# The first stage of a two-layer kernel rebuilt, and weight splits called ahead of unsplit blocks

## The chip, the cores and the metric

One core of a Trainium2 chip. The metric is the device time of one execution of the program in microseconds, the median of several runs. The kernel before takes 2598.72 us (three runs, 2596.58 to 2601.68).

## What is computed

Two transformer layers run one after the other over 512 tokens of width 1024, in float32. Only the start and the middle of the first layer matter here:

```python
mod = jax.nn.silu(c) @ w_ada[l] + b_ada[l]          # c: 1 x 1024, w_ada: 1024 x 6144
shift1, scale1, gate1, shift2, scale2, gate2 = jnp.split(mod[:, None, :], 6, axis=-1)
h = rms_norm(x, norm1_w[l]) * (1 + scale1) + shift1
proj = h @ w_in[l]                                   # split into q, k, v, z, alpha, beta, mla_*, gates
...
o_b = mla_attention(mla_q, mla_ckv, mla_kr, ...)     # keys and values from ckv @ w_uk, ckv @ w_uv
y_b = o_b.reshape(B, S, MLA_VD) @ w_out_mla[l]
```

The first 24 column blocks of `proj` (q, k and v of 8 heads, 128 columns each) go through a short causal convolution and silu into a gated delta rule; alpha and beta are its gates. MLA is latent attention: its keys and values come from a 256-wide latent through `w_uk` and `w_uv`. The rest of layer one (output products, gated FFN) and layer two follow.

## The kernel before

**Layout.** Activations lie channel-major: a tile is 128 channels x 512 tokens, 2 KB per partition, in an SBUF arena of 57 such tiles. A product of one output tile of 128 channels takes, for each of the eight 128-row slices k of the weight block, three TensorE matmuls in fp32r (`mm3`): weights and input are each split into a high half (rounded to fp32r) and a low half (the rest), and hi x hi, hi x lo and lo x hi are summed in PSUM. One block of 128 columns is 24 matmuls of 128x512.

**Weight blocks.** A block is 128 x 1024 floats (512 KB). The sync engine (SP) loads the blocks in the order of one list, `W.list`, into three raw slots (`RAW`). For a split block ScalarE copies raw to `WHI` (a 128x1024 activation), and VectorE (odd list numbers) or GpSimd (even ones) writes the difference to `WLO`; both have three buffers. A raw slot is free again when the low half is made. Some blocks are not split: 32 pieces of `w_ada` for parts 2 to 5, used by VectorE, and `w_uv` (2) and `w_uk` (8, one for each head), used raw by TensorE; their slot is free when they have been used. The list is made by running the same program once with a planner (`Plan`). In it, numbers 0 to 4 are ab (k_rope, alpha, beta), dn0, dn8, dn16, dn1, then w_ada pieces and dn blocks alternate (number 10 is dn2). Later come z0 at 71, 72, then uv0, uv1 (73, 74), z0 75, 76, z1 77 to 79, uk0, uk1 (80, 81), z1 82, gd 83, 84, uk2, uk3 (85, 86), gd 87 to 92, gm 93, uk4, uk5 (94, 95), gm 96 to 102, uk6, uk7 (103, 104), and ya (`w_out_dn`) from 105.

**Who splits when.** Every engine runs the same program of stages, each with its own steps, in order. A linear stage calls `self.ahead(i)` for each of its blocks i before anything else; ScalarE, VectorE and GpSimd then split all blocks of the list up to number i + 2 that are not split yet (lines 1533, 2205, 2868). ScalarE waits there for the raw block, and for the buffer that the third split block before has used. Only linear stages and the w_ada stages call it; the MLA steps with uv and uk blocks don't.

**The first stage** (`prologue` of each engine, lines 1014, 1558, 2224, 2889, and `sync_program`, line 3127). SP loads two pieces of constants, parts 0 and 1 of w_ada whole (8 MB in four loads of 2 MB), a third piece of constants, some 30 small vectors as rows, and then the list. ScalarE's queue loads c and x (2 MB). TensorE transposes x into eight channel-major tiles; VectorE copies each from PSUM (`XT`), ScalarE squares it, VectorE adds the squares; one product with ones gives the sum over channels, ScalarE takes its inverse root; GpSimd multiplies all eight tiles by it. VectorE takes silu(c) @ w_ada for parts 0 and 1 with 32 multiply-adds of 128x512, and `ada_end` sums over partitions on TensorE with 16 products by a column of ones. Then for each k the scaled and shifted tile is made (ScalarE for even k, VectorE for odd), split by ScalarE (high) and VectorE or GpSimd (low), and TensorE runs its first k-loop over two blocks at once, ab and dn0:

```python
lin("ab", w_in, 8, 0, 256, H1, lambda m: ("dn_ve", 0) if m else ("ab_act", "kr"), fresh=True, ...)
```

`fresh` makes the first two blocks of a linear stage share one k-loop, so that TensorE follows the input tiles as they are made. Behind it ScalarE splits block 3 and evicts ab (`ab`, `gates_ab`), convolutions and silus follow (`dn_conv`, `dn_taps`, `dn_silu`), then the loop over the other q, k and v blocks. ScalarE writes `XT` to memory (`xs1`) for the residual sum.

**The MLA part.** `beside` (linear stages z0, z1, gd, gm, gates, `split_o`, ya) is woven with `norms_then`: `mla_norms` with the uv products and the norms and rotations of q and k, then the heads in pairs (`mla_head`). A head's first step is its uk product on TensorE, a Square of it on ScalarE, an add on VectorE; its second is a product with ones, then logarithm, exponential and the scores. `split_o` makes the high and low halves (`HO`) that ya reads.

Of the kernel before, what the change touches and what calls it, by code (L numbers as in the profile page):

```python
# [7 lines left out]
P = 128  # L8
# [208 lines left out]
class Lin:  # L217


    def __init__(self, name, w, kn, c0, ncol, X, freed, m0=0, r0=0, parts=None, fresh=False):  # L220
# [65 lines left out]
def build(nc, D, out, known):  # L286
# [5 lines left out]
    with ctx:  # L292
# [90 lines left out]
        ADA0 = [A[:, 21 + 16 * i:37 + 16 * i, :].rearrange("p (k a) n -> p k (a n)", k=8) for i in range(2)]  # L383
# [24 lines left out]
        colpos, row_loads = {}, []  # L408
        g_, r_ = 0, 0
        for name, src, n, new in vectors:  # L410
# [3 lines left out]
            if name in ("qr", "kr"):  # L414
                row_loads += [(ROW[g_][r_:r_ + 1, 64 * hh:64 * hh + 64], src) for hh in range(2)]
            else:
                row_loads.append((ROW[g_][r_:r_ + n, :], src))
            r_ += n
# [47 lines left out]
        H1 = Split("h1", HP, lambda k: "po" if k % 4 == 1 else "ve")  # L466
# [21 lines left out]
        def lin(name, *a, **kw):  # L488
            L[name] = Lin(name, *a, **kw)

        lin("ab", w_in, 8, 0, 256, H1, lambda m: ("dn_ve", 0) if m else ("ab_act", "kr"), fresh=True,
            parts=lambda g: [(rows(w_in, 0, 8, MR, 64), 0), (rows(w_in, 0, 8, 4096, 32), 64),
                             (rows(w_in, 0, 8, 4104, 32), 96)] if g == 0 else [(rows(w_in, 0, 8, 0, P), 0)])
        for c in range(1, 24):
# [7 lines left out]
        lin("z0", w_in, 8, 3072, 512, H1, lambda m: ("z_ve", m))  # L502
        lin("z1", w_in, 8, 3584, 512, H1, lambda m: ("z_ve", m), m0=4)
        lin("gd", w_in, 8, GD, 1024, H1, lambda m: ("gd_ve", m))
        lin("gm", w_in, 8, GD + 1024, 1024, H1, lambda m: ("gm_ve", m))
        lin("ya", D["w_out_dn"][0], 8, 0, 1024, HO, lambda m: ("ya_ve", m))
        lin("yb", D["w_out_mla"][0], 8, 0, 1024, OB, lambda m: ("yb_ve", m), fresh=True)
        lin("wo", D["w_o"][0], 8, 0, 1024, HM, lambda m: ("r1_ve", m), fresh=True)
        lin("ple", D["w_ple_2"][0], 2, 0, 1024, PP, lambda m: ("ple_act", m))
        up_ = D["ffn_w_up"][0]  # L510
        lin("fu0", up_, 8, 0, 256, H2, lambda m: ("fv_ve", 0) if m else ("fa_ve", 0), fresh=True,
# [4 lines left out]
        lin("fd", D["ffn_w_down"][0], 22, 0, 1024, FP, lambda m: ("r2_ve", m))  # L516
        SU, SV, GQ, GK, GV, GR, GA, AQ, AK, AV, CA, CG = 0, 512, 1024, 1280, 1536, 2048, 2560, 2576, 3088, 3600, 4112, 4624
        lin("cv0", w2, 8, 0, 256, H3, lambda m: ("ca_ve", 0) if m else ("cg_act", 0), fresh=True,
# [5 lines left out]
        lin("aq", w2, 8, AQ, 512, H3, lambda m: ("aq_act", m))  # L524
        lin("ak", w2, 8, AK, 512, H3, lambda m: ("ak_act", m))
        lin("ga", w2, 8, GA, P, H3, lambda m: ("ga_act", m))
        lin("gk", w2, 8, GK, 256, H3, lambda m: ("gk_act", m))
        lin("gq", w2, 8, GQ, 256, H3, lambda m: ("gq_act", m))
        lin("gr", w2, 8, GR, 512, H3, lambda m: ("gr_act", m))
# [5 lines left out]
        lin("w2", D["w_out_2"][0], 8, 0, 1024, HG, lambda m: ("r3_ve", m), fresh=True)  # L535
        for p in range(4):
            lin(f"up{p}", D["w_ff1_2"][0], 8, p * 1024, 1024, H4, lambda m, p=p: ("f2_ve", p, m), fresh=p == 0)
            lin(f"do{p}", D["w_ff2_2"][0], 8, 0, 1024, F2[p], lambda m, p=p: ("r4_ve", p, m), r0=8 * p)
        lin("pg", D["w_ple_gate_2"][0], 8, 0, 1024, H5, lambda m: ("pg_ve", m), fresh=True)
# [34 lines left out]
        def ADA_SUM(p):  # L574
            return [A[:, 53, :], A[:, 54, :]] if p == 1 else [SCR[3], SCR[4]]
# [70 lines left out]
        class Stages:  # L646
# [47 lines left out]
            def ev_ab(self, m, bk):  # L694
                if m:
                    self.ev_dn(0)(m, bk)
# [2522 lines left out]
```

## Time and profile before

| | |
|---|---|
| median of three runs | 2598.72 us |
| the profiled execution | 2600.64 us, its span 2598.7 us |
| mean granted clock of TensorE | 0.942 of 2.4 GHz |
| busy: TensorE, VectorE, ScalarE, GpSimd | 2343.5, 1103.9, 928.4, 732.1 us |

The span goes from the first instruction to the last; some 2 us of the execution lie around it. PE is TensorE's matmuls, PEld its weight loads, DVE VectorE, ACT ScalarE, POOL GpSimd; SPq and ACTq are the queues that issue DMAs. `ps` is a PSUM bank, `wraw`, `whi`, `wlo` the weight buffers, `hhi`, `hlo` the input halves, `arena` and `scr` other tiles. Lines such as L342, L357 or L360 are helpers that issue every matmul, activation or tensor-tensor operation. In an arrow `a <- b` after an idle time, b is what the instruction waited for. A granted clock of 1.00 is 2.4 GHz, 0.50 is 1.2 GHz.

### The profile page before, as it was taken

To read this page: it belongs to the slowest core of one execution; us is meant where nothing else is said; L and a number is where in the kernel's file an instruction comes from. 1 tells how busy PE (TensorE), PEld (TensorE's weight loads), DVE (VectorE), ACT (ScalarE), POOL (GpSimd) and SP (SyncE) were. 2 spreads that over 40 slices of the span, in tenths; PEclk is the share of its full clock that TensorE was granted. 3 is DMA by queue.
4 is the path that set the end of the run, shared out by engine and by line. 5 is a ranking of instruction groups with operands and counts; after the bars stand their busy time and mean duration, and the time that the engine had idled before them with its cause. 6 is when DMAs were issued, how large, how long until landed. Compare 5 with 4: busy or idle time off the path is not lost.

```text
span 2598.7 us, 26841 instructions
## 1 busy us (share of the span) xinstructions
PE 2343.5 (90%) x10834; PEld 1895.1 (73%) x10834; DVE 1103.9 (42%) x1605; ACT 928.4 (36%) x1353; POOL 732.1 (28%) x427
## 2 busy tenths in 40 slices
PE   2788989997879989899999897999998999999996
PEld 2677877994457767688888685787776777888875
DVE  5466656444332333333331299613444243332333
ACT  2444424213342433433332332324553433422334
POOL 4341144101201025422232314221132343422332
PEclk6898989998889989999999898999999999999998
DMA  6321223131112123333333331232222322333331
GB/s 234 93 70 57 82 57 85 62 92 38 36 41 59 31 81 114 106 97 98 97 93 97 111 105 57 73 98 82 73 74 63 100 89 82 106 96 94 103 120 51
DMA packets 345822, 220.64 MB, mean 85 GB/s; under 512 B 18281, under 2 KB 327132, under 8 KB 345700
## 3 DMA queue, kind: packets, MB, share of 16 engines
q1 hardware_dynamic: 335940, 200.26, 26.5%
q10 hardware_dynamic: 9760, 18.67, 2.2%
q8 instruction: 87, 1.43, 0.2%
q14 instruction: 35, 0.29, 0.0%
HBM read 210.49 MB, written 8.41 MB: 84 GB/s over the span
## 4 chain that ended last, share of the span: by engine, by line
PE 74%; DVE 11%; ACT 8%; POOL 4%; issue 2%; DMA 1%; ACTq 0%; SPq 0%; DVEq 0%; POOLq 0%
PE ps L342 73%; DVE arena L368 4%; ACT arena L357 3%; DVE arena L360 2%; POOL arena L360 2%; ACT scr L357 1%; DVE scr L368 1%; ACT whi L357 1%; ACT L353 1%; POOL wlo L360 1%; PE ps L345 1%; DVE wlo L360 1%; DVE arena L365 1%; DMA arena<-in_x_dram 1%; DVE arena L371 0%
## 5 line engine op out<-in xcount | busy, mean ns | idle before, releaser
L342 PE MATMUL ps<-hhi,whi 128*128 128x512 f32 x1664 | 679.5, 408 | 81.0 <-POOL wlo L360 49.1
L360 POOL TENSOR_TENSOR wlo<-wraw,whi 128x1024 fp32r<-128x1024 f32 (+1 forms) x164 | 393.9, 2402 | 1144.2 <-ACT whi L357 1144.2
L342 PE MATMUL ps<-hlo,whi 128*128 128x512 f32 x1664 | 663.6, 399 | 0.0
L342 PE MATMUL ps<-hhi,wlo 128*128 128x512 f32 x1664 | 663.2, 399 | 0.0
L357 ACT ACTIVATE whi<-wraw 128x1024 fp32r<-128x1024 f32 (+1 forms) x328 | 340.8, 1040 | 375.6 <-PE ps L342 304.6
L342 PEld LDWEIGHTS ps<-hhi,whi 128*128 128x128 f32 x1664 | 323.2, 194 | 162.0 <-issue 78.2
L342 PE MATMUL ps<-arena 128*128 128x128 f32 (+4 forms) x2304 | 338.9, 303 | 42.1 <-ACT arena L357 17.8
L360 DVE TENSOR_TENSOR wlo<-wraw,whi 128x1024 fp32r<-128x1024 f32 x164 | 216.2, 1318 | 372.1 <-ACT whi L357 372.0
L342 PEld LDWEIGHTS ps<-hlo,whi 128*128 128x128 f32 x1664 | 323.3, 194 | 67.7 <-issue 2.9
L342 PEld LDWEIGHTS ps<-hhi,wlo 128*128 128x128 f32 x1664 | 321.4, 193 | 69.7
L342 PEld LDWEIGHTS ps<-arena 128*128 128x128 f32 x2304 | 290.8, 199 | 73.8 <-issue 21.7
L357 ACT ACTIVATE arena<-ps 128x512 f32<-128x512 f32 (+5 forms) x223 | 116.3, 540 | 350.3 <-PE ps L342 289.7
L342 PE MATMUL ps<-h,whi 128*128 128x512 f32 x512 | 160.3, 395 | 1.1 <-POOL wlo L360 1.1
L360 POOL TENSOR_TENSOR arena<-arena,scr 128x512 f32<-128x512 f32 x65 | 103.7, 1602 | 168.3 <-ACT scr L357 131.2
L368 DVE SCALAR_TENSOR_TENSOR arena<-arena,colv 128x512 f32<-128x512 f32 (+1 forms) x148 | 137.4, 935 | 30.4 <-ACT arena L357 26.7
L357 ACT ACTIVATE scr<-ps,colv 128x512 f32<-128x512 f32 x78 | 55.6, 712 | 253.4 <-PE ps L342 253.2
L368 DVE SCALAR_TENSOR_TENSOR scr<-ps,colv,scr 128x511 f32<-128x511 f32 (+2 forms) x116 | 86.9, 749 | 135.4 <-ACT scr L357 132.9
L360 DVE TENSOR_TENSOR arena<-ps,arena 128x512 f32<-128x512 f32 (+1 forms) x88 | 55.6, 639 | 149.8 <-PE ps L342 147.9
L360 DVE TENSOR_TENSOR scr<-ps,scr 128x512 f32<-128x512 f32 x86 | 59.1, 689 | 138.7 <-PE ps L342 137.1
L342 PE MATMUL ps<-arena,cst 128*128 128x512 f32 (+1 forms) x124 | 73.8, 725 | 45.5 <-ACT arena L357 18.9
L342 PEld LDWEIGHTS ps<-h,whi 128*128 128x128 f32 x512 | 97.3, 190 | 22.7 <-issue 2.6
L342 PE MATMUL ps<-ff,whi 128*128 128x512 f32 x352 | 108.4, 390 | 0.0
(192 smaller groups left out, 2680.8 us busy)
## 6 DMA issues: line engine op xcount, KB each, us to landing
wraw<-in_w_in_dram SPq DMA_DIRECT2D x99, 512.0 KB, 3.9
wraw<-in_w_ff_dram SPq DMA_DIRECT2D x64, 512.0 KB, 4.0
wraw<-in_ffn_w_up_dram SPq DMA_DIRECT2D x44, 512.0 KB, 3.9
wraw<-in_w_ada_dram SPq DMA_DIRECT2D x32, 512.0 KB, 4.0
wraw<-in_w_gate_dram SPq DMA_DIRECT2D x32, 512.0 KB, 3.6
arena<-in_w_ada_dram SPq DMA_DIRECT2D x4, 2048.0 KB, 20.1
wraw<-in_ffn_w_down_dram SPq DMA_DIRECT2D x16, 512.0 KB, 3.7
wraw<-in_w_branch_dram SPq DMA_DIRECT2D x16, 512.0 KB, 3.4
```

What stands on the lines that cost most here:

```text
L342: return pe.e.matmul(o, l, r, start=start, stop=stop)
L345: return pe.e.transpose(o, i, CST[0:n, C_ID:C_ID + n])
L353: ac.e.preload_act_table_set("natural_log_exp_and_others")
L357: return ac.e.activation(o, i, f, bias=bias, scale=scale, **kw)
L360: return q.e.tensor_tensor(o, a, b, op)
L365: return q.e.tensor_scalar(o, a, s1, s2, op0, op1)
L368: return ve.e.scalar_tensor_tensor(out=o, in0=a, scalar=s, in1=b, op0=op0, op1=op1)
```

## The change

**The first stage.** x is loaded by SP right after the first constants, in four loads of 128 tokens, each with its own semaphore. The w_ada parts 0 and 1 are loaded in two halves of 4 MB (half s holds columns 512 s to 512 s + 511 of both parts, in four loads); the first three weight blocks lie between the halves, and the small vectors, the third piece of constants and the rest of the list behind them. The nine row vectors that stand in the first row tile (b_ada and norm weights; `row_group` 0) go over ScalarE's queue. The mean square is taken token-major: ScalarE squares x with an accumulated sum per token, and ScalarE and VectorE scale two token tiles each by the inverse root, in place. x is transposed twice: unscaled for the residual, scaled (`turn_x`) for the layer. VectorE's 32 multiply-adds and GpSimd's eight multiplications go; w_ada is multiplied on TensorE as rows (weights: one column of silu(c), 512 columns stream), copied by VectorE, and turned to columns by eight products with a 1x1 one. VectorE makes every shifted tile straight from PSUM and every low half. The first k-loop has three blocks (ab, dn0, dn8), and the second w_ada half and its turns lie inside it, before k = 4; the other four row tiles are turned before k = 6. Block 1's low half is made behind the first half's mod. The write of x to memory moves behind high half 3.

**Splits ahead.** `mla_norms` and `mla_head` of ScalarE, VectorE and GpSimd call `ahead` for their uv and uk blocks, so the two blocks behind are split before that step.

**Names.** Semaphores of one engine are merged (`on_act`, `zg_act`, `gt_act`, `gs_act` into `mix_act`, and others alike); their order is the program's.

```diff
-        first = 2 if self.fresh else 1
+        first = self.fresh or 1
...
-        H1 = Split("h1", HP, lambda k: "po" if k % 4 == 1 else "ve")
+        H1 = Split("h1", HP, lambda k: "ve")
...
-        lin("ab", w_in, 8, 0, 256, H1, lambda m: ("dn_ve", 0) if m else ("ab_act", "kr"), fresh=True,
+        lin("ab", w_in, 8, 0, 384, H1, lambda m: ("dn_ve", 8 * m - 8) if m else ("ab_act", "kr"), fresh=3,
...
...
+            def ada_half(self, s):
+                for p in range(2):
+                    bk = PA.take("ar", s, p)
...
+                    for k in range(8):
+                        pe.wait_ge(SG.sem(f"ada_in{s}{p}{k // 4}"), 16)
+                        t = mm(bk[0:1, :], SC[:, k:k + 1], ADA0[s][p][:, k, :], k == 0, k == 7)
...
+                self.turn_x(4 * s)
+                self.turn_x(4 * s + 1)
...
+                for p in range(2):
+                    pe.wait_ge(*at("row_ve", s, p))
+                    for c in range(4):
+                        t = mm(bk[:, 4 * p + c:4 * p + c + 1], ADA_ROW[p][:, c * P:(c + 1) * P], ones[0:1, 0:1], True, True)
...
+                self.turn_x(4 * s + 2)
+                self.turn_x(4 * s + 3)
+            def between(self, k):
+                if k == 4:
+                    self.ada_half(1)
+                if k == 6:
...
...
+                ve.wait_ge(*at("st_act", "ri"))
+                for b in (0, 2):
+                    ts(ve, X0[:, b, :], X0[:, b, :], RX[:, b:b + 1], None, ALU.mult).then_inc(*inc("st_ve", "x", b))
...
+                for s in range(2):
+                    self.first_mod(s)
+                    if s == 0:
+                        self.ahead(0)
+                    for k in range(4 * s, 4 * s + 4):
...
+                        ts(ve, HS[k % 3], PA.of("hx", k)[:, :], modcol(1, k), modcol(0, k), ALU.mult, ALU.add).then_inc(
...
+                        self.low(H1, k, HS[k % 3])
...
+                    act(SCRT[:, 2 * (b % 2):2 * (b % 2) + 2, :].rearrange("p a n -> p (a n)"), X0[:, b, :], ACT.Square,
+                        accum=SQ4[:, b:b + 1]).then_inc(*inc("st_act", "sq", b))
...
+                for b in (1, 3):
+                    act(X0[:, b, :], X0[:, b, :], ACT.Copy, scale=RX[:, b:b + 1]).then_inc(*inc("st_act", "x", b))
+                self.ahead(0)
...
+                for n in range(2):
+                    self.ahead(W.index["uv", n])
...
             def mla_head(self, h):
+                self.ahead(W.index["uk", h])
...
+            for b in range(4):
+                sp.e.dma_start(X0[:, b, :], D["x"][0, b * P:(b + 1) * P, :]).then_inc(SG.sem(f"x_in{b}"), 16)
+            load_ada(0)
+            for u in W.list[0:3]:
+                load_block(u)
+            load_ada(1)
```

## Rows read from the trace of the kernel before

**Rows 1.** The page, part 1: busy us (share of the span), instructions.
```profile
PE 2343.5 (90%) x10834; PEld 1895.1 (73%) x10834; DVE 1103.9 (42%) x1605; ACT 928.4 (36%) x1353; POOL 732.1 (28%) x427
```

**Rows 2.** Table of stretches: us, PE, PEld, DVE, ACT, POOL busy (instructions), granted clock, DMA share, GB/s.
```profile
0.00:66.00 66.00, 17.01 (x72) 14.59 (x72) 39.75 (x58) 15.25 (x21) 31.13 (x16) 0.68 0.68 230
...
80.00:121.00 41.00, 30.66 (x134) 24.78 (x134) 23.35 (x31) 19.73 (x28) 9.82 (x4) 0.89 0.29 86
...
600.00:925.00 325.00, 264.19 (x989) 179.39 (x988) 121.95 (x225) 127.46 (x225) 49.92 (x27) 0.88 0.16 44
...
925.00:2598.00 1673.00, 1570.26 (x6892) 1278.36 (x6890) 648.03 (x869) 600.42 (x835) 519.21 (x294) 0.97 0.31 91
```

**Rows 3.** Chain of waits, 0 to 140 us, the longest pieces: start us, us, what.
```profile
1.36 13.35 DMA arena<-in_x_dram
...
35.71 27.09 POOL arena L360 x8
...
66.72 12.60 PE ps L342 x45
...
120.38 8.29 PE ps L342 x24
```

**Rows 4.** The same table of stretches, short stretches.
```profile
24.00:27.00 3.00, 0.00 (x0) 0.00 (x0) 2.19 (x4) 0.71 (x2) 0.00 (x0) 0.50 1.03 410
...
40.00:44.00 4.00, 3.57 (x16) 3.48 (x16) 4.00 (x8) 0.06 (x1) 4.00 (x1) 0.50 1.09 297
...
105.70:111.10 5.40, 5.40 (x25) 4.50 (x24) 4.52 (x5) 2.14 (x3) 2.40 (x1) 1.00 0.01 3
```

**Rows 5.** Timeline, TensorE: start us, us, what, form, count.
```profile
14.75 6.25 PE L345 MATMUL ps<-cst,arena 128*128 128x128 f32 x32 [11.33 <-DMA arena<-in_x_dram]
...
40.23 3.57 PE L342 MATMUL ps<-cst,scr 128*128 128x1 f32 x16 [3.15 <-DVE scr L368]
```

**Rows 6.** Timeline, VectorE and GpSimd: a copy from PSUM, a low half.
```profile
15.90 0.69 DVE L371 COPY arena<-ps 128x512 f32<-128x512 f32 x1 [15.90 <-PE ps L345]
...
75.61 2.40 POOL L360 TENSOR_TENSOR wlo<-wraw,whi 128x1024 fp32r<-128x1024 f32 x1 [1.17 <-ACT whi L357]
```

**Rows 7.** TensorE's forms, 200 to 260 us: ns min/median/max, first and last start.
```profile
L342 PE MATMUL ps<-hhi,whi x32: 388/390/794, 199.8 to 259.7; 128*128 128x512 f32 x32
...
L342 PE MATMUL ps<-arena,cst x8: 593/593/593, 224.9 to 227.9; 128*128 128x512 f32 x8
```

**Rows 8.** Timeline, ScalarE behind the first two blocks.
```profile
79.41 1.06 ACT L357 ACTIVATE whi<-wraw 128x1024 fp32r<-128x1024 f32 x1 [3.87 <-PE ps L342]
...
93.17 1.15 ACT L357 ACTIVATE gb<-arena 40x512 fp32r<-40x512 f32 x2 [2.50 <-DVE arena L2294]
...
98.77 1.04 ACT L357 ACTIVATE whi<-wraw 128x1024 fp32r<-128x1024 f32 x1
```

**Rows 9.** Timeline, ScalarE, VectorE and the sync queue around the unsplit blocks.
```profile
616.70 1.23 DVE L360 TENSOR_TENSOR wlo<-wraw,whi 128x1024 fp32r<-128x1024 f32 x1 [5.92 <-ACT whi L357]
...
698.31 0.37 SPq L3146 DMA_DIRECT2D wraw<-in_w_in_dram  x1
...
700.52 1.05 ACT L357 ACTIVATE whi<-wraw 128x1024 fp32r<-128x1024 f32 x1
...
702.20 1.06 ACT L357 ACTIVATE whi<-wraw 128x1024 fp32r<-128x1024 f32 x1 [0.63 <-DMA wraw<-in_w_in_dram]
...
896.37 26.93 SPq L3146 DMA_DIRECT2D wraw<-in_w_out_dn_dram  x4
...
911.47 4.25 ACT L357 ACTIVATE hhi<-arena 128x512 fp32r<-128x512 f32 x8
```

**Rows 10.** Waits of TensorE, 600 to 930 us (us, times, longest); one from the timeline.
```profile
PE ps L342 <- DVE wlo L360: 14.5, 3, 9.5
...
PE ps L342 <- POOL wlo L360: 8.3, 2, 4.1
...
704.14 0.76 PE L342 MATMUL ps<-hhi,whi 128*128 128x512 f32 x1 [4.14 <-POOL wlo L360]
```

More of the change, by code:

```diff
@@ L811, in program @@
             first = f.qkv(more)
-            for _ in range(5):
+            for _ in range(4):
                 next(first)
@@ L1027, in prologue @@
                     PA.put(("xt", k), "st_ve", "xt", k)
-                bk = PA.take("ri")
-                pe.wait_ge(*PA.free("ri"))
-                pe.wait_ge(*at("st_ve", "sum", 7))
-                mm(bk[:, :], ones, SQT, True, True).then_inc(*inc("st_mm", "ri"))
-                PA.put(("ri",), "st_act", "ln")
-                pe.wait_ge(SG.sem("rows"), 16 * len(row_loads))
-                pe.wait_ge(*at("st_po", "rz"))
+                pe.wait_ge(SG.sem("rows0"), 16 * row_group.count(0))
@@ new lines, in turn_x @@
+            def turn_x(self, k):
+                bk = PA.take("hx", k)
+                pe.wait_ge(*PA.free("hx", k))
+                pe.wait_ge(*at("st_ve", "x", 2))
+                pe.wait_ge(*at("st_act", "x", 3))
+                for b in range(4):
+                    t = tr(bk[:, b * P:(b + 1) * P], X0[:, b, k * P:(k + 1) * P])
+                t.then_inc(*inc("st_mm", "h", k))
+                PA.put(("hx", k), "st_ve", "h", k)
+            def between(self, k):
+                if k == 4:
+                    self.ada_half(1)
+                if k == 6:
+                    pe.wait_ge(SG.sem("rows"), 16 * (len(row_loads) - row_group.count(0)))
+                    bk = PA.take("col1")
+                    pe.wait_ge(*PA.free("col1"))
+                    for i in range(4):
+                        t = tr(bk[:, i * P:(i + 1) * P], ROW[1 + i])
+                    t.then_inc(*inc("st_mm", "col1"))
+                    PA.put(("col1",), "st_ve", "col1")
@@ L2426, in mla_norms @@
                 for n in range(2):
+                    self.ahead(W.index["uv", n])
                     for p in SG.ends("rec"):
@@ L2965, in mla_norms @@
             def mla_norms(self):
-                for _ in range(8):
+                yield
+                yield
+                for n in range(2):
+                    self.ahead(W.index["uv", n])
+                    yield
+                for _ in range(4):
                     yield
@@ L2977, in mla_norms, with mla_head @@
                 yield
-            mla_head, o_norms, z_gate, gates = Plan.idle_head, Plan.o_norms, Plan.z_gate, Plan.gates
+            def mla_head(self, h):
+                self.ahead(W.index["uk", h])
+                for _ in range(11):
+                    yield
+            o_norms, z_gate, gates = Plan.o_norms, Plan.z_gate, Plan.gates
             def split_o(self):
@@ L3124, in ev_pg, with load_ada, load_block @@
                     self.add_square("pg", m, [A[:, 32, :], A[:, 33, :]])
+        def load_ada(s):
+            for p in range(2):
+                for g in range(2):
+                    sp.e.dma_start(ADA0[s][p][:, 4 * g:4 * g + 4, :],
+                                   rows(D["w_ada"][0], 4 * g, 4, p * 1024 + s * S, S)).then_inc(SG.sem(f"ada_in{s}{p}{g}"), 16)
+        def load_block(u):
+            if u["before"] is not None:
+                sp.wait_ge(*at(*raw_free(u["before"])))
+            v = raw_of(u["i"])[:, 0:u["kk"] * u["n"]].rearrange("p (k n) -> p k n", k=u["kk"])
+            for src, off in u["parts"]:
+                sp.e.dma_start(v[:, :, off:off + src.shape[2]], src).then_inc(SG.sem(f"raw{u['slot']}"), 16)
         def sync_program():
```

331 lines of the change are left out of this document (160 added, 171 removed).

## The prediction

> **What bounds the kernel now.** I read the engine table first: TensorE is busy 90% of the span, the next engine 42% [rows 1]. So a microsecond is only to be had where TensorE waits. The table of stretches says where that is: TensorE is busy for 17.0 of the first 66 us, 30.7 of the 41 us from 80 to 121, and 264 of the 325 from 600 [rows 2]. The change works in these stretches. The rest stays as it is, and moves as a block.
>
> In the first stage the chain of waits goes through the load of x (13.4 us), a ping-pong of copies, squares and sums, eight multiplications on GpSimd (27.1 us), and only at 66.7 us into the first product [rows 3]. The two blocks of the first k-loop end near 80.0 us (the row shows the first block's end; the second's last three matmuls come 0.7 us later). From there to the eleventh block (number 10 of the list) at 120.4 TensorE starts a block only when it has been loaded and split: a raw slot comes free, the block lands, is split, and only then used. So after the first stage the pace is that of load and split, and an earlier start moves this chain as a whole.
>
> **Part 1, the first stage, step by step.** x is alone at the head of the queue. The queue moves 410 GB/s in its 2 MB loads [rows 4], so 2.1 MB from about 3 us (the old x load began at 1.4 us; two constant loads and four issues lie ahead) are in at about 8.5 us, and the first half of w_ada (4.2 MB, 10.2 us) at 19; 10.7 by a shorter 2 KB row is no matter, as TensorE is later. The three weight blocks and the second half follow at 25 and 36 us. The 32 transposes took 6.25 us, but in the old ping-pong [rows 5]; unbroken copies of 0.69 us each [rows 6] don't hold them back, so 7 us: 15.5. The squares, the logarithm and the scaling (four passes of 1.05 us on ScalarE as the 128x1024 split, two on VectorE) end at 18.4, beside TensorE. The nine row loads now on ScalarE's queue, some 0.3 us each, are issued by 5 us and queue only ScalarE's first square behind them.
>
> TensorE then takes w_ada as 16 products of 128x512 for each half, 32 instructions. The nearest row is the ones product in full fp32: eight instructions starting 3.0 us from first to last, 0.43 us apart at 2.4 GHz [rows 7]; at 1.2 GHz, half of it, they are 0.86 apart, which is the other bound. I take 0.43, as the transposes ahead of them leave the engine busy: 13.7 us, to 29.5. Four transposes, eight column products and the row copies, as 16 instructions that took 3.57 us at 1.2 GHz [rows 5], halved, and 16 transposes: 3.9 us, to 33.4. VectorE's bias and gain (0.6), its split of block 1 (1.2) and the first turned block (product from PSUM 0.65, ScalarE 0.65, subtraction 0.7) put the first product at 36.5. Each k needs 9 matmuls, and 25 took 5.4 us [rows 4], 2.04 us, and on VectorE and ScalarE 2.09, so four take 8.2, plus 2.5 for a restart at half clock: 47.1. The second half lies on the path now, since TensorE is in order: 13.7 and 3.9 to 64.7, then 1.8 for the first block, four k of 2.09, and the 0.5 of the column transposes: 75.4, or 76 with some half clock. So **three blocks are done at 76, where two were done at 80.0**.
>
> What comes after loses part of that. ScalarE's split of block 3 started at 79.41, as the first pair's loop ended; the gates' work followed, and the split of block 6 came at 98.77 [rows 8]. Now there are two splits ahead of the gate work instead of one (1.05), and ahead of it too one more convolution with three taps on VectorE (2.3) and a silu that waits for them (1.9 with its table); 1.2 come back, as block 3 may be split 1.2 us before the loop ends. Worked through in ScalarE's order, block 6 is split 19.5 us after the loop, subtracted by 23.0 (2.4 on GpSimd [rows 6]), block 8 loads (4.5; such a load alone took 3.9 from issue to split [rows 9]), is split and subtracted by 31.0, and block 10 by 39.1: 115.1 us, against a start at 120.4 [rows 3]. **Part 1 gives 5.3 us**; the third block taken early buys nothing beyond, as it only fills the wait behind it. With the loop's end between 71 and 84 this is +10 to -3.
>
> TensorE's clock decides this part. In the stretch from 40 to 44 us it was busy 3.57 of 4 us with one-column products and stayed at the lower level, 1.2 GHz [rows 4]. The new row products are one column wide on the other side: their weights are a single column, and 512 columns stream. No row shows such a product. The Trainium skill, "TensorE: Matmul & The Clock Gate" (section on the HAM clock gate), says that the clock depends on how busy the engine has been, with the lower level as the default. By the page the sum has 13.7 us for a half; by the row from 40 to 44, if it is what counts, 27.3.
>
> **Part 2, splits ahead of unsplit blocks.** Five times between 600 and 925 us TensorE waits for a low half: 2.01, 4.14, 2.98, 4.15 and 9.52 us, three for VectorE's and two for GpSimd's [rows 10]. Each lies right behind a pair of unsplit blocks (w_uv, then w_uk of two heads): the split of the next block was asked for only by that block. The raw data was there: at the second wait ScalarE's split starts at 700.52 with no wait for a load [rows 9]. The new calls take it before the pair.
>
> First wait: the low half is made before the copies, TensorE starts at 608.9 and saves 2.0; VectorE then also waited 5.92 us, until 616.7, for the next block [rows 9], whose slot came free late. That slot is now free before the pair, so the copy behind the split, at 617.9, follows the product instead (608.9 + 5.5 = 614.4): **3.5**. Second: 4.1 for the wait and 1.8 for the restart at half clock (its first matmul took 0.76 us [rows 10], where the median is 0.39 [rows 7]): **5.9**. Third, which started nearly warm: **3.0**. Fourth: 4.15 and 0.7, **4.8**. Cost: in the second head of each pair ScalarE now waits for a block whose slot that pair frees (issued at 698.31, split from 702.20 [rows 9]) with its Square behind it; that is 3.2 us later, but TensorE has a block of 5.5 us to do meanwhile. At the fifth wait there is no such block: the load issued at 896.37 [rows 9] lands near 900.3, Square waits, and heads 6 and 7 lose 3.1 us. Then the eight highs that started at 911.47 [rows 9] start at 914.6, and the products of w_out_dn start behind the first low, near 916, and go at the pace of GpSimd's lows to 922.8. Before, that first block ran from 920.27 for 5.5 us and 1.8 of restart, to 927.6: **4.8** net. Together **22.0 us**.
>
> The merged semaphores (on, z, zg, gd, gm and so on) are counted by one engine in program order as before; they issue nothing new and cost nothing.
>
> What is moved past queues stays covered. The other small loads and the last 612 KB of constants now follow the second half on the sync queue and are in by some 42 us; GpSimd's two casts wait for them, and behind those only memsets that are due at 76. The write of x to memory leaves ScalarE's queue at the fifth block (some 43 us), holds one issue, and is due only when a silu first writes over x, past 90. Block 3's product needs a bank that ScalarE's copies free 4.6 us after the loop; its successor, block 6, waits for its split until 23 us, so this costs nothing unless that wait goes.
>
> **Sum.** 27.3 us off the profiled execution's 2600.64 gives 2573.3; it stood 1.9 us above the median of 2598.72, so the median goes to about 2572. Later stages are limited by TensorE (busy 1570 of 1673 us [rows 2]) and hide no earlier start.
>
> **Rivals.** *(a) The row products run at 1.2 GHz.* Two halves cost 27.3 instead of 13.7 us, and their transposes and column products 3.6 more each: 34 us, all on TensorE's path. Net +7: 2606. It decides when some four fifths of both halves run low. For it: the stretch from 40 to 44. Against: there the data streamed was one column in 0.22 us, here 512. *(b) ScalarE's new waits cost as much as they save.* Its queue is in order, so the wait for the second block's load delays both heads' exponentials; if TensorE's block does not cover it, the second to the fifth wait return half: 11 instead of 22, so 2583. *(c) The calls do nothing:* the slot or the high buffer is still taken when they are reached, and ScalarE stands there instead. Part 2 is nothing: 2593. Against it: the split at 700.52 waited for neither.
>
> **How the numbers follow.** Forecast 0.59, (a) 0.13, (b) 0.18, (c) 0.10. Part 1 between +10 and -3 and part 2 between 11 and 25 put the range at 2562 to 2590; with (c) and a part of (a)'s way it reaches 2594, and 2560 below. About 0.2% (5 us) is what a measurement of this kernel can tell from no change: faster 0.82, the same 0.06 (halves of (a) and (c)), slower 0.12.
>
> **What would show it.** Right: x landed by 9 us, first product near 36, a gap of some 18 us in the k-loop with 32 row matmuls 0.43 apart at a granted clock near 1, three blocks done near 76, block 10 near 115; no wait over 1 us for a low half behind uk or uv. Wrong: row matmuls 0.86 apart; first product after 45; Squares of odd heads late with TensorE waiting for them; or the five waits still there under another name.

## The result, and the profile after

The kernel after takes 2569.65 us (median of four, 2568.42 to 2577.01) against 2599.32 us (median of four) of the kernel before: the ratio is 0.9892, with a 95% interval of 0.9871 to 0.9913, so 29.7 us or 1.1% faster. The forecast was 2572, inside a range of 2560 to 2594. The profiled execution took 2570.07 us, with a span of 2568.3. Below it will turn out that the total is better than its parts: one part gave more than forecast, the other less.

The page, part 1, of the kernel after; it answers to [rows 1]:
```profile
PE 2358.6 (92%) x10928; PEld 1890.4 (74%) x10928; DVE 1083.0 (42%) x1579; ACT 927.7 (36%) x1352; POOL 700.4 (27%) x417
```
TensorE is busy for 15 us more and the span is 30 us shorter: the row products of w_ada are new work on the engine that bounds the kernel, put where it stood idle. The table of stretches of the kernel after shows where, against [rows 2] (us, then PE, PEld, DVE, ACT, POOL busy, granted clock, DMA share, GB/s):
```profile
0.00:66.00 66.00, 51.78 (x199) 26.07 (x200) 18.67 (x31) 16.12 (x23) 8.41 (x12) 0.93 0.79 254
...
595.00:892.00 297.00, 249.06 (x969) 171.57 (x968) 117.16 (x219) 125.97 (x224) 46.30 (x26) 0.91 0.18 46
892.00:2568.00 1676.00, 1568.58 (x6893) 1275.81 (x6891) 650.87 (x870) 600.43 (x834) 519.48 (x296) 0.97 0.31 90
```
In the first 66 us TensorE is busy for 51.8 instead of 17.0. From the first unsplit block to the products of w_out_dn the idle time falls from 61 to 48 us. The last stretch is as long as before, within 3 us.

The chain of waits of the kernel after, its long pieces in the first 120 us, answers to [rows 3]:
```profile
3.08 6.45 DMA arena<-in_x_dram
9.66 5.33 PE ps L345 x33
14.99 13.82 PE ps L342 x32
...
35.65 24.35 PE ps L342 x68
60.00 1.03 PE ps L345 x8
61.03 1.88 PE ps L342 x16
...
65.81 6.73 PE ps L342 x18
72.97 2.78 PE ps L342 x12
...
112.22 2.46 POOL wlo L360
114.82 5.74 PE ps L342 x24
```
Read it from the bottom. Block 10 starts at 114.82 where it started at 120.38, and its 24 products take 5.74 us where they took 8.29. Only the first of these two differences was in the forecast. TensorE's wait just ahead of the block is now short (timeline):
```profile
114.82 0.47 PE L342 MATMUL ps<-hhi,whi 128*128 128x512 f32 x1 [0.50 <-POOL wlo L360]
```

To follow a gain along the kernel I take the start of ScalarE's high half of a block in each trace and subtract that of the kernel before. For after: 5.7 us earlier at block 10, 8.1 at block 14, 8.7 at block 27, 10.1 at block 31, 13.0 at block 57, and 13.0 still at block 75, where the first unsplit block comes. From there it rises to 31.9 at block 109 and ends at 31.1.

### The profile page after: what moved, and what is told of

Read it like the earlier page. It is cut to its first block, busy times and chain, and to the rows that moved or that the text cites. A ratio compares the mean times of both kernels' runs of the same rounds, so it can differ in the third digit from the quotient of the medians.

```text
span 2568.3 us, 27012 instructions
## 1 busy us (share of the span) xinstructions
PE 2358.6 (92%) x10928; PEld 1890.4 (74%) x10928; DVE 1083.0 (42%) x1579; ACT 927.7 (36%) x1352; POOL 700.4 (27%) x417
## 4 chain that ended last, share of the span: by engine, by line
PE 75%; DVE 11%; ACT 8%; POOL 3%; issue 3%; DMA 1%; ACTq 0%; SPq 0%; DVEq 0%; POOLq 0%
PE ps L342 74%; DVE arena L368 4%; ACT arena L357 4%; DVE arena L360 2%; DVE scr L368 1%; PE ps L345 1%; ACT scr L357 1%; POOL wlo L360 1%; ACT whi L357 1%; ACT L353 1%; POOL arena L360 1%; DVE arena L365 1%; DVE scr L360 1%; DVE wlo L360 1%; DMA wraw<-in_w_in_dram 1%
## 5 line engine op out<-in xcount | busy, mean ns | idle before, releaser
L360 POOL TENSOR_TENSOR arena<-arena,scr 128x512 f32<-128x512 f32 x57 | 76.5, 1346 | 133.8 <-ACT scr L357 96.8
L342 PE MATMUL ps<-arena,cst 128*128 128x512 f32 (+1 forms) x122 | 70.1, 703 | 34.5 <-ACT arena L357 17.7
```

Of the source, the lines that this page charges most:

```text
L342: return pe.e.matmul(o, l, r, start=start, stop=stop)
L360: return q.e.tensor_tensor(o, a, b, op)
```

## The experiments

Expectations are quoted as they stood before each run. Medians are against runs of the kernel before on the same chip. Positions inside a kernel are from its one profile.

**1. The first stage alone.** The three classes lose their calls ahead of w_uv and w_uk:
```diff
-                    self.ahead(W.index["uv", n])
-                self.ahead(W.index["uk", h])
```


> The first stage alone: the kernel after, without the calls ahead of w_uv and w_uk. Theory G (the gain of the first stage grows behind block 10, because TensorE reaches block 10 almost without a stop and stays at 2.4 GHz): block 10 starts near 114.8 us, everything from about 450 us on is 13 us earlier than before, and the time is 12 to 13 us below before, near 2587. Rival F (the forecast's sum, in which the shift of the first stage stays 5.3 us, and what the traces show beyond it belongs to the calls or to chance): 5.3 us below before, near 2594. The waits for low halves between 600 and 925 us are there as before, 19 to 24 us in all by the profile's waits.

Measured: 2589.45 us against 2597.59; the ratio 0.9969 [0.9958, 0.9980] is 8 us, between 5 and 11. In the trace block 10 is 5.1 us earlier than before, block 14 7.6, block 57 12.5, block 109 13.7. So what grows behind block 10 belongs to the first stage, as theory G has it; the median of six runs gives 8, not the 13 of the profile. The 5.5 us between lie in which executions were profiled: that of before took 3.0 us more than the median of before here (2600.64 against 2597.59), and that of run 1 was the fastest of its six, 2.5 us below their median. Runs 11 and 12 show how two executions of one program come to differ by that much.

**2. The calls alone**, added to the kernel before.

> The calls ahead of w_uv and w_uk alone, in the kernel before. Theory G: nothing moves before 600 us, then 19 us are gained up to about 890 us: near 2580. Rival F: the forecast's 22 us or the 24 that are left of the measured gain when the first stage gives 5.3: 2575 to 2577. A third possibility is that the two parts are not additive (the calls profit from where the first stage puts the blocks): then less than 15 us, above 2584.

Measured: 2584.40 us, ratio 0.9949 [0.9936, 0.9962]: 13 us, between 10 and 17. In its trace nothing moves before 590 us (0.9 us later), and at block 109 it is 17.0 earlier: 17.9 from the calls. The medians of the two parts add up to 21.3 us, with some 3 us of uncertainty each, the whole measured 29.7 and 28.8. The traces show no piece that only both together give (after minus run 1 is 18.2 at block 109, run 2 gave 17.9), so I take the two parts as additive. The medians do not show it: they fall 7 to 8 us short of the whole, and that gap stays open.

**3. Two blocks in the first k-loop.**
```diff
-        lin("ab", w_in, 8, 0, 384, H1, lambda m: ("dn_ve", 8 * m - 8) if m else ("ab_act", "kr"), fresh=3,
+        lin("ab", w_in, 8, 0, 256, H1, lambda m: ("dn_ve", 0) if m else ("ab_act", "kr"), fresh=2,
...
-        for c in (*range(1, 8), *range(9, 24)):
+        for c in range(1, 24):
```


> The kernel after with only two blocks in the first k-loop; the third is an ordinary block behind it. The forecast's claim (the third block taken early buys nothing, since it only fills the wait for the split of block 6): block 10 starts within 1 us of 114.8, and the time is that of the kernel after within 2 us, near 2570. Rival: the third block's 24 products ride at the pace of VectorE inside the loop and cost TensorE nothing there, so as an ordinary block it costs its full 5.5 us behind the loop: near 2575; and if TensorE then comes late to block 10 the start moves to 117 or later.

Measured: 2571.24 us, ratio 0.9902 [0.9886, 0.9918], that of after within the intervals. The loop ends 3.4 us earlier, block 10 is split at 110.6 instead of 111.1. As far as the start of block 10 goes the forecast's claim holds: the third block taken early buys nothing there, because TensorE waits 4.16 us for block 6 in the kernel after. But it decides where TensorE waits. With two blocks in the loop the stop ahead of block 10 is back, and the clock with it (timeline of TensorE, run 3):
```profile
114.22 0.77 PE L342 MATMUL ps<-hhi,whi 128*128 128x512 f32 x1 [2.98 <-POOL wlo L360]
114.78 0.63 PE L342 MATMUL ps<-hlo,whi 128*128 128x512 f32 x1
```
The block's 24 products take 7.16 us here, 5.74 in the kernel after. From block 10 to block 14 the gain on the kernel before grows by 0.5 us in this run, and by 2.4 to 2.5 in all the executions of the six that run 11 lists. So this growth comes with the third block. What it is worth in the end is less: block 14 is 6.6 us earlier in run 3 and 7.1 in the mean of the six, and the medians cannot tell the two apart.

**4. Fourteen of the second half's row products left out.**
```diff
-                        t = mm(bk[0:1, :], SC[:, k:k + 1], ADA0[s][p][:, k, :], k == 0, k == 7)
+                        if s == 0 or k == 7:
+                            t = mm(bk[0:1, :], SC[:, k:k + 1], ADA0[s][p][:, k, :], k == 0 or s == 1, k == 7)
```


> The kernel after with only the last of the eight products for each part of w_ada in the second half (14 of 16 are left out, so the bias and gain of the last four blocks of x are wrong sums): 14 x 0.86 = 12.0 us less on TensorE in the gap of the first k-loop. The forecast's claim (the second half lies on TensorE's path, and the chain behind it moves as a whole): the loop ends near 64 us, block 10 starts near 103, and the time is 12 us below the kernel after, near 2558. Rival: the second half of w_ada lands and the splits of VectorE and ScalarE go at a pace of their own, so the loop ends only some 6 us earlier and the time is near 2564. Second rival: the loop ends 12 us earlier, but the loads of the blocks behind it, or ScalarE's gate work, hold the chain, and less than half of it reaches block 10.

Measured: 2557.84 us, ratio 0.9849 [0.9833, 0.9864]; 11.8 less than the kernel after. Block 3 is split 12.0 us earlier than in after (63.8 for 75.8), block 10 12.3 earlier. Both rivals fall. The row products are on the path that sets the stage, and the chain of load and split behind it moves as a whole.

**5. The odd head's call behind its norm.**
```diff
-                self.ahead(W.index["uk", h])
+                if e == 0:
+                    self.ahead(W.index["uk", h])
...
                 act(SCR[e], SCR[e], ACT.Exp, scale=-0.5).then_inc(*inc("ma_act", "ri", h))
+                if e == 1:
+                    self.ahead(W.index["uk", h])
```
and so behind KZ on VectorE.

> The kernel after, with the call ahead of w_uk of an odd head moved behind the exponential of its key norm (ScalarE) and behind the rotated key's product (VectorE), so that neither head's Square and logarithm wait for the next block's load. Forecast's mechanism (the call costs 3.1 us at heads 6 and 7; the trace of after shows ScalarE waiting 3.83 us for w_out_dn at 870.93 and TensorE 5.97 us behind it): everything from the first product of w_out_dn on is 3 to 4 us earlier than in the kernel after, near 2566.5, and TensorE's wait at 875 shrinks to 2 us or less. Rival: TensorE waits for the chain of norms of two heads anyway (with nothing else to do there), and the wait only changes its name: under 1 us, near 2570.

Measured: 2564.58 us, ratio 0.9860 [0.9845, 0.9874], 5.1 below after. What it removes stands in the kernel after, heads 6 and 7, timeline of TensorE and ScalarE:
```profile
864.59 3.60 PE L342 MATMUL ps<-arena,wraw 128*128 128x512 f32 x8
...
870.93 1.06 ACT L357 ACTIVATE whi<-wraw 128x1024 fp32r<-128x1024 f32 x1 [3.83 <-DMA wraw<-in_w_out_dn_dram]
871.89 0.58 ACT L357 ACTIVATE scr<-ps 128x512 f32<-128x512 f32 x1
...
875.01 2.07 PE L342 MATMUL ps<-scr,cst 128*128 128x512 f32 x2 [5.97 <-DVE scr L360]
```
ScalarE stands at the split of w_out_dn's block until it lands; head 7's Square (871.89) is behind it, and TensorE waits 5.97 us for what follows. The wait names VectorE's sum, but the DMA set it. In the timeline of run 5 the same product comes 1.58 us after the one of head 6, the Square at 866.87, the split at 871.51 without a wait:
```profile
866.67 1.02 PE L342 MATMUL ps<-scr,cst 128*128 128x512 f32 x2
868.25 1.12 PE L342 MATMUL ps<-scr,cst 128*128 128x512 f32 x2 [0.56 <-DVE scr L360]
```
The products of w_out_dn start 5.0 us earlier (882.69 for 887.68); relative to the blocks ahead of w_uv, where this run is 0.6 behind after, it is 6.2 ahead at block 109, and 2.0 of them are there by block 91, behind the third pair. The rival (only the name changes) falls.

**6. Eight row products of the second half ahead of the first k.**
```diff
             def ada_half(self, s):
-                for p in range(2):
+                for p in range(s, 2):
+                    self.ada_rows(s, p)
...
             def between(self, k):
+                if k == 0:
+                    self.ada_rows(1, 0)
```
`ada_rows(s, p)` is the eight products of one part with their bank.

> The kernel after, with the eight row products of the shift part of w_ada's second half (6.9 us) ahead of the first k instead of in the gap at the fifth. They fill TensorE's wait of 2.92 us for the first low half and keep it busy, so the first k steps run at 2.4 instead of 1.2 GHz. Theory (TensorE's path sets this stage): the first product starts near 39.6 instead of 35.65, k = 0 to 3 take 8.3 instead of 10.5 us, the loop ends 4 to 5 us earlier, and block 10 too: near 2565. Rival: the first four k go at the pace of VectorE and ScalarE (2.09 us each) and are not late at present, or the data of the second half is not there at 32.7: less than 1.5 us gained, near 2569, or a loss up to 3 us.

Measured: 2570.01 us, ratio 0.9876 [0.9859, 0.9892]: nothing gained. The loop ends 2.6 us earlier, and so is block 10 (2.4). Timeline of TensorE in this run:
```profile
34.46 8.35 PE L342 MATMUL ps<-arena,mod 128*1 128x512 f32 x16 [1.37 <-DVE scr L365]
42.73 0.50 PE L342 MATMUL ps<-hhi,whi 128*128 128x512 f32 x1
```
The products waited 1.37 us for a bank that VectorE frees, started at the lower clock (8.35 us instead of 6.9: the first instructions stand 0.81 to 0.85 us apart, those from the fifth on 0.43), and so put the first k at 42.7, not 39.6; from there the four k took the expected 8.3 us. The 2.4 us were lost again at places far behind: 1.2 at block 16, 1.6 at block 31, 2.8 at block 57. I had no reason for that until run 11.

**7. Constants multiplied ahead of block 10's wait**, in the kernel before.
```diff
+            def fill(self, key, bk):
+                for _ in range(FILL.get(key, 0)):
+                    mm(bk[:, 0:256], ones, CST[:, 0:256], True, True)
```
with 7 for block 10, called ahead of the wait for the block's weights.

> The kernel before, with seven products of constants (128x256, some 3.0 us at 2.4 GHz) issued ahead of TensorE's 3.02 us wait for block 10, into the bank that block 10 then overwrites. Theory (2.5 us of the first stage's gain, and 1.7 in the sums behind, are not earlier work but the clock: block 10 starts without a stop and so at 2.4 GHz): block 10 still starts near 120.4, its 24 products take 5.7 instead of 8.3 us, and block 14 is split 2.5 to 4.2 us earlier than before. Rival: the clock does not follow from the pause ahead of block 10 but from the slower stretch before it, or the chain behind goes at the pace of load and split: block 10 takes 8 us as before, or block 14's split does not move.

Measured: 2593.18 us, ratio 0.9972 [0.9961, 0.9984], 7 us faster than before, between 4 and 10. TensorE's timeline in the kernel before, at block 10:
```profile
120.38 0.77 PE L342 MATMUL ps<-hhi,whi 128*128 128x512 f32 x1 [3.02 <-POOL wlo L360]
120.94 0.63 PE L342 MATMUL ps<-hlo,whi 128*128 128x512 f32 x1
```
and in run 7:
```profile
117.09 3.29 PE L342 MATMUL ps<-cst 128*128 128x256 f32 x14
120.13 0.48 PE L342 MATMUL ps<-hhi,whi 128*128 128x512 f32 x1
120.45 0.39 PE L342 MATMUL ps<-hlo,whi 128*128 128x512 f32 x1
```
The start is the same within 0.3 us, the matmuls take 0.39 instead of 0.63 us, and block 14 is split 2.2 us earlier, block 16 3.0. So at this place the pause decides the clock of what follows it, and this is worth 2 to 3 us. The median gives 7, which is more than this place can explain: the trace has another 2.7 us between blocks 50 and 57, in the stretch near 430 us that run 11 takes up.

**8. The same ahead of nine waits of the kernel after** (3 to 14 products, in the bank of the block that waits).

> The kernel after, with products of constants ahead of nine waits of TensorE for a low half (3 to 14 of 0.43 us each, sized to end before the wait does), into the bank that the block then overwrites. Seven of the waits are followed by blocks that now start at 1.2 GHz and lose 2 to 3 us each. Theory as in the run before: 12 to 17 us below the kernel after, near 2555. Rival: the products are late themselves or the clock stays low behind them: no gain, or up to 5 us slower.

Measured: 2576.42 us, ratio 0.9905 [0.9890, 0.9920]; 6.8 above the first median of after and 5.0 above the second (run 11), though the intervals of the ratios overlap. The 12 to 17 us expected are not there. The theory was too simple in two ways. At two of the nine places TensorE waits for the *bank* first, so the constants come when the wait is over and at the lower clock. In the timeline this is (kernel after, then run 8)
```profile
2019.02 0.76 PE L342 MATMUL ps<-hhi,whi 128*128 128x512 f32 x1 [5.41 <-POOL wlo L360]
```
```profile
2022.23 7.26 PE L342 MATMUL ps<-cst 128*128 128x256 f32 x22 [4.62 <-ACT scr L357]
2029.14 0.58 PE L342 MATMUL ps<-hhi,whi 128*128 128x512 f32 x1
```
which cost 4.2 us; the other place, ahead of the second block of w_up, gave nothing. And in the first stage, where the pace is that of load and split, block 6 done faster only made TensorE wait for block 8 (1.81 us, nothing gained by block 12), and the restarts behind it then fell otherwise than in after: 2.0 us later by block 16, 3.0 by block 31, 6.0 by block 57. Ahead of the second block of w_o the run gains 2.5 us on the first execution of after, but that does not show that the constants pay: run 11, without them, gains the same there behind the same wait. First matmul of the block, the kernel after and then run 11:
```profile
1000.80 0.77 PE L342 MATMUL ps<-hhi,whi 128*128 128x512 f32 x1 [3.50 <-POOL wlo L360]
```
```profile
1006.60 0.47 PE L342 MATMUL ps<-hhi,whi 128*128 128x512 f32 x1 [3.50 <-POOL wlo L360]
```
The only place where constants are shown to pay is block 10 of run 7.

**9. GpSimd's low half ahead of its last rotation.**
```diff
                 for j in range(4):
                     yield
                     yield
+                    if j == 3:
+                        self.ahead(W.index["uk", 0])
                     self.rope(j, QR[j])
```


> The kernel after, with GpSimd's call ahead of the first w_uk moved in front of its last rotation, so that the low half of the block behind the second pair is made at about 675.5 to 678 us and not at 682.4 to 685.1. Theory (the second wait gave 2.2 us and not the forecast's 5.9, because GpSimd stands in the rotation, which waits for TensorE's product at 679.5, while the high half has been there since 675.5): TensorE starts the block near 683.2 without a stop and at 2.4 GHz; 3.5 to 4 us less than the kernel after from there on, near 2566. Rival: the chain of norms of heads 0 and 1 (TensorE waits for it right behind that block) sets the time there, and the gain is given back at that wait: under 1 us, near 2569.5.

Measured: 2567.85 us, ratio 0.9876 [0.9863, 0.9890]; 3.6 below the kernel after as run on the same chip (run 11), with intervals that overlap (0.9879 to 0.9906 for after), so the trace has to carry it. GpSimd in the kernel after, timeline:
```profile
679.78 1.26 POOL L360 TENSOR_TENSOR arena<-arena 128x512 f32<-128x512 f32 x1 [14.48 <-PE ps L342]
681.13 1.26 POOL L360 TENSOR_TENSOR arena<-arena,scr 128x512 f32<-128x512 f32 x1
682.35 2.79 POOL L360 TENSOR_TENSOR wlo<-wraw,whi 128x1024 fp32r<-128x1024 f32 x1
```
and in run 9:
```profile
676.03 2.80 POOL L360 TENSOR_TENSOR wlo<-wraw,whi 128x1024 fp32r<-128x1024 f32 x1 [10.37 <-ACT whi L357]
680.23 1.27 POOL L360 TENSOR_TENSOR arena<-arena 128x512 f32<-128x512 f32 x1 [1.40 <-PE ps L342]
```
GpSimd had stood idle for 14.48 us with the high half there from 675.5. TensorE starts the block at 683.01 instead of 685.28 and at 2.4 GHz, though it is 0.5 us behind in the blocks before. From block 75 to block 88 this run gains 4.6 us on after, by either execution of after; one comes back at the fifth wait.

**10. Both, 5 and 9 together.**

> GpSimd's low half ahead of the last rotation and the calls of the odd heads behind their norms, both in the kernel after. If the two are independent, the sum of both: some 5 us of the latter (measured) and 3.5 to 4 of the former, near 2561. Rival: they share the waits of heads 0 and 1, and the sum is that of the larger one alone, near 2565.

Measured: 2561.41 us, ratio 0.9854 [0.9841, 0.9867]; 10.0 below the kernel after on the same chip (run 11), with intervals that don't overlap (0.9879 to 0.9906 for after). The single gains are 3.6 (run 9) and 5.1 by the medians or 6.2 by the trace (run 5), together 8.7 to 9.8, so the rival falls: they are independent. This is the fastest version, 1.5% below the kernel before.

**11 and 12. The kernels after and before once more, unchanged.**

> The kernel after once more, unchanged. The first profile of after is 1.4 us better against before from 260 us on and 2.6 us better from 440 us on, with the same work and the same pauses there and another granted clock. Theory L (the granted clock behind two short pauses differs from execution to execution): this profile differs from the first at one or both places by 1.3 to 2.8 us, although the blocks before them start at the same times within 0.7 us. Rival P (the program decides it): both stretches have the same granted clock and the blocks the same times within 0.7 us all along.

> The kernel before once more, unchanged. Theory L: as for the kernel after; the stretch from 424 to 448 us may run at 1.00 this time instead of 0.88, and then everything behind it is 2.6 us earlier. Rival P: 0.88 again, the same times within 0.7 us. By both, block 10 starts behind a 3 us stop at 1.2 GHz and takes 8 us again, since that stop is no matter of chance.

Measured: after 2571.46 us, ratio 0.9892 [0.9879, 0.9906], the first result again; before 2596.41 against 2600.29, ratio 0.9990 [0.9981, 0.9999], which is how far the same kernel can be from itself: 3.9 us, by an interval that excludes 1. The traces decide for L. One program, two executions; timeline of TensorE, the kernel after the first time:
```profile
413.12 1.16 PE L342 MATMUL ps<-arena 128*128 128x128 f32 x8 [1.15 <-DVE arena L365]
414.21 0.49 PE L342 MATMUL ps<-gb,sel 40*128 40x512 f32 x1
414.63 1.23 PE L345 MATMUL ps<-cst,arena 128*128 128x128 f32 x8
415.61 0.49 PE L342 MATMUL ps<-hhi,whi 128*128 128x512 f32 x1
```
and the second time:
```profile
415.35 2.08 PE L342 MATMUL ps<-arena 128*128 128x128 f32 x8 [1.15 <-DVE arena L365]
417.35 0.79 PE L342 MATMUL ps<-gb,sel 40*128 40x512 f32 x1
418.07 1.97 PE L345 MATMUL ps<-cst,arena 128*128 128x128 f32 x8
419.69 0.78 PE L342 MATMUL ps<-hhi,whi 128*128 128x512 f32 x1
```
The same instructions behind the same pause of 1.15 us: once at 2.4 GHz, once at 1.2. It costs 2.6 us by block 57. Nor is it only short pauses: behind the 3.5 us wait at w_o shown under run 8, which every execution without the constants has, the next split comes 9.9 us after the block's start in runs 3, 6 and 11, and in run 8 with its constants, 11.5 us in the kernel before and six others, and 12.4 to 12.5 in after, run 2 and run 9. The kernel before shows the like near 245 us (table of stretches, first profile, then run 12):
```profile
240.00:246.00 6.00, 6.00 (x16) 4.71 (x16) 4.54 (x5) 0.00 (x0) 3.48 (x5) 0.56 0.23 71
```
```profile
240.00:246.00 6.00, 4.65 (x25) 3.73 (x23) 4.93 (x6) 2.16 (x3) 2.42 (x3) 1.00 0.38 114
```
and is 3.4 us earlier from block 29 on in the second. The stop ahead of block 10 is no matter of chance: runs 2 and 12 have it too (2.97 and 2.99 us), and restart at 1.2 GHz. Not all that differs is the clock behind pauses: run 11 is 2.3 us behind the first execution at block 10 already, 1.0 of it because its first transposes took 6.34 instead of 5.33 us.

What the first stage is worth is then to be read over several executions. Six have it new with the rest of that stage unchanged (after, runs 1, 5, 9, 10, 11), three have it old (before, runs 2, 12). Mean start against the first profile of before:
```
            new (six)    old (three)   difference
block 10      -4.6          -0.1          4.5
block 14      -7.1          -0.1          7.1
block 71     -11.6          -1.2         10.4
```
(by block, for the new: 5.7, 5.1, 5.0, 4.9, 3.9, 3.3 earlier at block 10; 8.1, 7.6, 7.5, 7.4, 6.4, 5.9 at block 14; 13.0, 12.5, 12.4, 12.5, 11.2, 8.2 at block 71).

## Why the prediction was right, and where it was not

**What bounds the kernel** held with one gap: TensorE's waits were to be had, but also the half-clock restarts behind them, which the engine table counts as busy time. The stages behind w_out_dn moved as a block as forecast (their length is that of before within 3 us).

**The first stage up to block 10** held nearly term by term. x was in at 9.5 us (8.5 forecast; the load took 6.45 us). The transposes took 5.3 (7), and ended at 15.0 (15.5). The rows took 13.89 for 32 instructions (13.7). The first product was at 35.65 (36.5); the fifth k at 65.8 (66.5). The first block of the loop was done at 75.75 and ScalarE split block 3 at 75.83 (76); block 10 started at 114.8 (115.1). Run 4 confirmed the claim that the second half lies on the path, run 3 the one that the third block does not start block 10 earlier. One step did not add up as written: 33.4 and the terms behind it give 37.2, not 36.5, for the first product; and nine of 25 matmuls in 5.4 us are 1.94 us, not 2.04. Neither moves the sum by more than a microsecond. Over six executions block 10 is 4.5 us earlier, for the 5.3 of the sum.

**Rival (a)**, rows at 1.2 GHz, is refuted: the 32 instructions stand 0.43 us apart. The forecast leaned on the transposes ahead of them leaving the engine busy, and run 6 shows the other side: behind a pause of 1.37 us sixteen of them took 8.35 us. The Trainium skill, "TensorE: Matmul & The Clock Gate" (section on the HAM clock gate), has the clock follow how busy the engine has been; by that rule the trace agrees here.

**"Part 1 gives 5.3 us" is the step that failed**, as the gain of the whole stage. It took the shift at block 10 for the shift of all that follows. The price of the pause was in [rows 3], in the 8.29 us for 24 products that take 5.74 at 2.4 GHz: in the kernel before TensorE stood 3.02 us ahead of block 10 and restarted at half clock, in the new one it waits 0.50 us and does not. Run 3 shows what does this: not the earlier start, but the third block in the loop, of which the prediction said that it "only fills the wait behind it". It does not only fill a wait, it moves the stop from block 10 to block 6: without it TensorE stops 2.98 us ahead of block 10 and restarts low, as before. I had counted such restarts in part 2 and forgot to ask the same of the last wait of part 1. That makes 4.5 into 7.1 by block 14, and run 7 shows the cause alone (2.2 to 3.0 us). The other 3.3 us up to block 71 come at pauses that both kernels have. In part they are chance (run 11 lost 2.6 of it, run 12 won 3.4). The stretch near 420 us ran high in five of the six executions with the new stage, and low in the three with the old. But it ran high too in run 7, which has the old stage, and low in runs 4, 6 and 8, which have variants of the new one. So whether the new stage favours this is open.

**Part 2 gave 18.2 us of the forecast's 22.0**, and by single waits less evenly than that. After minus run 1, which differ only in the calls:
```
wait          forecast   measured (at block)
first            3.5        3.3  (79)
second           5.9        2.1  (84)
third            3.0        3.9  (91)
fourth           4.8        6.9  (100)
fifth            4.8        2.0  (109)
```
Of the first wait's 3.3 us 0.4 stood between the two traces before the first unsplit block; 17.7 are left for the calls, and run 2 has 17.9.

*Second*: the step "4.1 for the wait and 1.8 for the restart" assumed that the low half follows the high. It was GpSimd's, and in GpSimd's order it stands behind a rotation that waits for TensorE. The high half started at 674.5, the low one only at 682.35, and TensorE kept a wait of 2.14 us and the restart. Run 9 gives this back. I had named the queues that the change moves things past, but not the one that the new call itself joins. *Fourth*: the restart was put at 0.7 by its first matmuls; it cost 2.0, as the block took 7.83 us before (834.38 to 842.21) and 5.87 after (806.50 to 812.37). *Fifth*: the cost of 3.1 for the wait for the load was the right mechanism, and measured 3.83 on ScalarE and 5.97 on TensorE; run 5 gives it back. About 1 us more went at w_o in this execution; by run 11 that is the clock behind a wait, and not the calls' doing.

**Rival (b)**, ScalarE's waits eat half of part 2: its place was right (the fifth wait), its size not, as at the other pairs TensorE did have a block to do; only at heads 2 and 3 it waited as well, 2.1 us. **Rival (c)**, the calls do nothing, is refuted by run 2. Of the 22.8 us of waits for a low half in [rows 10] (14.5 and 8.3) 2.1 are left. Waits of TensorE, 595 to 892 us of the kernel after (us, times, longest):
```profile
PE ps L342 <- DVE scr L360: 8.1, 2, 6.0
...
PE ps L342 <- POOL wlo L360: 2.1, 1, 2.1
```
The second line is the second wait, halved. The first was 0.6 in the kernel before, and is now the fifth wait under another name, with 2.1 at the norm of heads 2 and 3.

So the total of 27.3 came within 2.4 us of the measured 29.7 because an omission in part 1 and too much in part 2 cancel. That the total is so close is luck. The chances of "same" and "slower" stood the wrong way round: halves of (a) and (c) are 0.12 for the same, and 0.06 was left for slower.

## What to carry to other kernels

When a wait of the bounding engine is shortened, look at each pause behind it and at the clock of the block that follows: the restart of a block at block 10 cost 2.6 us here, behind a pause of 3.0. Filling one wait can move the stop to another place, as the third block did. A call that takes work forward joins a queue on every engine that has a part of that work; look at what stands ahead of it on the slowest of them, and put it behind whatever must not wait for its load. And a gain of a few microseconds read from one profile against another is no firmer than the clock behind a pause, 1 to 3 us at a place; read it over several executions.

## What the runs showed of the hardware that was not expected

The granted clock behind the same pauses differs between executions of one program: two pauses of 1.06 and 1.15 us in 6 us left 2.4 GHz in one execution of the kernel after and 1.2 GHz in the other, 2.6 us of difference; in the kernel before 3.4 us at another place. At w_o even a wait of 3.50 us, the same in all executions, was followed by 2.4 GHz from the first matmuls on in run 11 and by 1.2 GHz for twelve matmuls in the kernel after, 2.5 us of difference. The Trainium skill, on the page named above and in its section on the HAM clock gate, says that the number of slow matmuls of a kernel changes from run to run; the trace agrees, and shows it in the middle of a kernel, not only at its start. Products whose weights are one column (128x512 streamed) kept the clock up, where the one-column streams of the kernel before had stayed at 1.2 GHz for their 3.57 us [rows 4]. Those had started at the lower clock behind a pause of 3.15 us, so the two are not quite alike; run 6 has the nearer case, where the same row products started low behind a pause of 1.37 us and stood 0.43 us apart from the fifth on.
